# Stick-breaking attention: a head pair's weighted sums on both array column halves, logits on both row halves

## The reference

```python
kb, vb = k_sh[:, :, :end], v_sh[:, :, :end]
logits = jnp.einsum("bhtd,bhsd->bhts", q[:, :, s0:end], kb) * (Dh ** -0.5)
mask = s_idx[None, :] < t_idx[:, None]
log_keep = jnp.where(mask, jax.nn.log_sigmoid(-logits), 0.0)
after = jnp.sum(log_keep, axis=-1, keepdims=True) - jnp.cumsum(log_keep, axis=-1)
wts = jnp.where(mask, jnp.exp(jax.nn.log_sigmoid(logits) + after), 0.0)
outs.append(jnp.einsum("bhts,bhsd->bhtd", wts, vb))
```

## Time and profile before

| | us |
|---|---|
| median of 3 runs | 1438.62 |
| lowest, highest | 1436.43, 1439.15 |
| span of the profiled execution | 1436.6 |
| the attention, first logits to the last weighted sum | 769.5 to 916.0 |

### The profile page before, as it was taken

One profiled execution on the slowest core, in us unless ns is written; L12 is line 12 of the kernel. 1 busy time (PEld: TensorE's weight loads), 2 busy tenths in 40 slices (PEclk: granted clock), 3 DMA queues, 4 the chain that ended last, 5 costly groups with the idle time before them and its releaser, 6 DMA issues.

```text
span 1436.6 us, 17837 instructions
## 1 busy us (share of the span) xinstructions
PE 1348.6 (94%) x7266; PEld 1037.2 (72%) x7266; DVE 472.6 (33%) x844; ACT 565.2 (39%) x926; POOL 398.5 (28%) x162
## 2 busy tenths in 40 slices
PE   6699999999999988999998999898999999999979
PEld 3588867789888866777775555676887777777747
DVE  0755532342342321334221333213112233242541
ACT  3343458432233522344344566323313434553410
POOL 0343431311124443233332000033223313335131
PEclk9899999999999989999999999999999999999969
DMA  9333311234442012222312000022213321224001
GB/s 334 110 88 104 100 59 59 89 118 147 137 129 89 2 59 88 71 85 83 109 64 88 0 0 1 1 88 94 88 53 109 93 70 60 88 71 179 16 0 59
DMA packets 102978, 117.82 MB, mean 82 GB/s; under 512 B 4560, under 2 KB 88944, under 8 KB 102904
## 3 DMA queue, kind: packets, MB, share of 16 engines
q1 hardware_dynamic: 98640, 112.21, 24.0%
q10 hardware_dynamic: 4264, 4.57, 1.1%
HBM read 111.52 MB, written 2.10 MB: 79 GB/s over the span
## 4 chain that ended last, share of the span: by engine, by line
PE 86%; ACT 6%; DVE 5%; issue 2%; ACTq 0%; DMA 0%; DVEq 0%
PE ps L1541 46%; PE ps L1635 4%; PE ps L2054 3%; PE ps L1769 3%; PE ps L1917 3%; PE ps L1784 3%; PE ps L1930 2%; PE ps L1903 2%; PE ps L1782 2%; PE ps L1624 2%; PE ps L1920 2%; PE ps L2023 1%; PE ps L1851 1%; PE ps L1846 1%; PE ps L2010 1%
## 5 line engine op out<-in xcount | busy, mean ns | idle before, releaser
L427 POOL TENSOR_TENSOR wlo<-raw,whi 128x2048 fp32r<-128x2048 f32 x58 | 267.2, 4607 | 697.5 <-ACT whi L550 685.1
L550 ACT ACTIVATE whi<-raw 128x2048 fp32r<-128x2048 f32 x56 | 106.9, 1911 | 264.6 <-PE ps L1541 229.6
L1635 PE MATMUL ps<-work,cs 128*128 128x512 f32 x160 | 78.4, 610 | 4.3 <-ACT work L555 4.1
L578 ACT ACTIVATE rbuf<-ps,cs 128x512 f32<-128x512 f32 x59 | 40.0, 679 | 63.4 <-PE ps L1635 48.7
L435 POOL TENSOR_TENSOR wlo<-raw,whi 128x2048 fp32r<-128x2048 f32 x10 | 46.3, 4634 | 66.8 <-ACT whi L614 66.8
L1314 DVE SCALAR_TENSOR_TENSOR nlk<-ps,att 128x1280 f32<-128x1280 f32 x16 | 23.9, 1492 | 118.9 <-ACT att L851 118.9
L444 POOL COPY yib<-cs 128x512 f32<-128x512 f32 x40 | 24.1, 615 | 122.6 <-PE ps L1784 122.6
L1784 PE MATMUL ps<-XT,yib 128*128 128x128 f32 x320 | 57.7, 276 | 0.0
L1541 PE MATMUL ps<-hC_hi,whi 128*128 128x512 f32 x208 | 55.1, 407 | 0.0
L939 ACT ACTIVATE p<-sc,nmx 128x256 f32<-128x256 f32 x64 | 32.1, 502 | 57.8 <-DVE nmx L1382 57.8
L1917 PE MATMUL ps<-nlk,cs 128*128 128x512 f32 (+3 forms) x128 | 48.1, 458 | 6.0 <-DVE after L1324 6.0
(11 more groups left out here) (367 smaller groups left out, 2972.1 us busy)
## 6 DMA issues: line engine op xcount, KB each, us to landing
raw<-in_w_in_dram SPq DMA_DIRECT2D x24, 1024.0 KB, 5.2
raw<-in_w_in_a_dram SPq DMA_DIRECT2D x16, 1024.0 KB, 5.6
raw<-in_w_ada_dram SPq DMA_DIRECT2D x16, 1024.0 KB, 5.2
raw<-in_w_ada_kv_dram SPq DMA_DIRECT2D x8, 1024.0 KB, 5.5
raw<-in_w_kv_dram SPq DMA_DIRECT2D x8, 1024.0 KB, 5.2
raw<-in_w_in_b_dram SPq DMA_DIRECT2D x8, 1024.0 KB, 5.4
ada_a<-in_w_ada_dram SPq DMA_DIRECT2D x4, 1024.0 KB, 8.3
ada_b<-in_w_ada_dram SPq DMA_DIRECT2D x4, 1024.0 KB, 10.7
```

The costliest lines, as they stand in the source:

```text
L427: pool.tensor_tensor(wlo[:, s, :], raw[:, s, :], whi[:, s, :].bitcast(F32), ALU.subtract).then_inc(lo_ready, 1)
L550: A(whi[:, s, :], raw[:, s, :], ACT.Copy).then_inc(hi_ready, 1)
L578: A(rbuf[:, g % 2, :], ssbank(g), ACT.Ln, scale=1.0 / width, bias=epsc).then_inc(ss_read, 1)
L1635: mm(ssbank(g), stat, work4[:, n % 4, :], start=first, stop=last).then_inc(sq_used, 1)
```

## The change

- `weighted` now takes a pair: for each j the product of the even head and then that of the odd head. It is called on odd n alone, `weighted((n - 3) // 2)`, and counts pairs in `pv_full`. `att` has four buffers instead of three, and the waits on `pv_full` on ScalarE and VectorE follow.
- New tiles `swk`, `swq` hold, for the pair at hand and in two buffers, the keys of blocks 1 and 3 and the queries from 128 on with the partition halves exchanged. SP copies them there with four DMA transfers for a pair (64 KB of keys and 96 KB of queries for each half), `swap(kt)`, after the load of half 0 of `D_OUTB + 1` and before that of half 1.
- `qk` computes blocks j = 0 and 2 on the head's own row half and j = 1 and 3 on the other half from the copies, in the order 0, 1, 2, 3. It waits for the copies, and once for both weights of head n - 2 before j = 0.
- Memory: `att`, `nlk1`, `after0` and `after1` now lie over half 1 of `whi` and `wlo`. So half 1 of `D_OUTB` is split after the attention: ScalarE's `next_hi(D_ZB + 1, 1)` moves behind the loop, ahead of the last `yb_hi`; POOL waits for 7 pairs before its part; SP's load of half 1 of `D_OUTB + 1` waits for that.

```diff
+            def swap(kt):
+
+                sp.wait_ge(kqn_done, 8 + kt + 1)
+                sp.wait_ge(dense_full, 4 * (D_VB + 2))
+                if kt >= 2:
+                    sp.wait_ge(qk_full, 2 * (kt - 2) + 2)
+                for e in range(2):
+                    to, of = slice(64 * e, 64 * e + 64), slice(64 - 64 * e, 128 - 64 * e)
+                    sp.dma_start(swk[to, kt % 2, :, :],
+                                 kTb[of, kt, :].rearrange("p (a two n) -> p a two n", two=2, n=128)[:, :, 1, :]
+                                 ).then_inc(swapped[kt % 2], 16)
+                    sp.dma_start(swq[to, kt % 2, :], qTb[of, kt, 128:512]).then_inc(swapped[kt % 2], 16)
...
+                if r == load_of["dense", D_OUTB + 1]:
+                    load(r, (0,))
+                    for kt in range(KD):
+                        swap(kt)
+                    load(r, (1,))
+                    continue
...
                 for s in range(2):
+                    if (d, s) == (D_OUTB, 1):
+                        pool.wait_ge(pv_full, KD - 1)
                     split_lo(d, s)
...
-            copies(D_ZB + 1, lambda j: zsT[:, 4 + j, :], gate_done, ACT.Silu)
+            next_hi(D_ZB + 1, 0)
+            for j in range(4):
+                act.wait_ge(dense_full, 4 * (D_ZB + 1) + j + 1)
+                A(zsT[:, 4 + j, :], dense[j], ACT.Silu).then_inc(gate_done, 1)
...
             def head_exps(n):
-                a = att[:, n % 3, :]
+                a = att[:, n % 4, :]
                 act.wait_ge(qk_full, n + 1)
-                if n >= 3:
-                    act.wait_ge(pv_full, n - 2)
+                if n >= 4:
+                    act.wait_ge(pv_full, (n - 4) // 2 + 1)
...
+            next_hi(D_ZB + 1, 1)
             yb_hi(KD - 1)
...
             def qk(n):
-                s, kt, rs = n % 2, n // 2, slice(64 * (n % 2), 64 * (n % 2) + 64)
-                for j in (0, 1, 3, 2):
-                    if n >= 2 and j < 2:
-                        pe.wait_ge(wt_done, 2 * (n - 2) + 1 + j)
-                    last = mm(logit_cols(s, off[j], 512 - 128 * j), kTb[rs, kt, 128 * j:128 * j + 128],
-                              qTb[rs, kt, 128 * j:512], start=j != 3, stop=True, skip_group_check=True)
+                s, kt = n % 2, n // 2
+                rs, other = slice(64 * s, 64 * s + 64), slice(64 - 64 * s, 128 - 64 * s)
+                pe.wait_ge(swapped[kt % 2], 64 * (kt // 2 + 1))
+                if n >= 2:
+                    pe.wait_ge(wt_done, 2 * (n - 2) + 2)
+                for j in (0, 1, 2, 3):
+                    if j % 2:
+                        k, q = swk[other, kt % 2, j // 2, :], swq[other, kt % 2, 128 * j - 128:384]
+                    else:
+                        k, q = kTb[rs, kt, 128 * j:128 * j + 128], qTb[rs, kt, 128 * j:512]
+                    last = mm(logit_cols(s, off[j], 512 - 128 * j), k, q, start=j != 3, stop=True,
+                              skip_group_check=True)
...
-            def weighted(n):
-                s, kt, rs = n % 2, n // 2, slice(64 * (n % 2), 64 * (n % 2) + 64)
-                pe.wait_ge(wt_done, 2 * n + 2)
-                if kt >= 2 and n % 2 == 0:
+            def weighted(kt):
+                pe.wait_ge(wt_done, 4 * kt + 4)
+                if kt >= 2:
                     pe.wait_ge(yb_done, kt - 1)
                 for j in range(NT):
-                    last = mm(ps[rs, 6 + kt % 2, 128 * j:512], Vb[:, j, 64 * n:64 * n + 64],
-                              att[:, n % 3, off[j]:off[j] + 512 - 128 * j], start=j == 0, stop=True, skip_group_check=True)
+                    for n in (2 * kt, 2 * kt + 1):
+                        rs = slice(64 * (n % 2), 64 * (n % 2) + 64)
+                        last = mm(ps[rs, 6 + kt % 2, 128 * j:512], Vb[:, j, 64 * n:64 * n + 64],
+                                  att[:, n % 4, off[j]:off[j] + 512 - 128 * j], start=j == 0, stop=True,
+                                  skip_group_check=True)
                 last.then_inc(pv_full, 1)
...
-                if n >= 2:
-                    weighted(n - 2)
+                if n >= 3 and n % 2:
+                    weighted((n - 3) // 2)
                 if n + 1 < HB:
                     qk(n + 1)
```

More of the change, by code:

```diff
@@ L137, in mixer_stack @@
             with ExitStack() as s2:
-                att = sb("att", [128, 3, 1280], F32, s2)
-                after1 = sb("after1", [128, 256], F32, s2)
-            with ExitStack() as s2:
                 sc2 = sb("sc2", [128, 2, 512], F32, s2)
@@ L157, in mixer_stack @@
             kbg = sb("kbg", [128, 2, 4, 128], F32, scope)
+        with ExitStack() as scope:
+            sb("pad_w0", [128, 2048], F32, scope)
+            nlk1 = sb("nlk1", [128, 1280], F32, scope)
+            after0 = sb("after0", [128, 384], F32, scope)
+            sb("pad_w1", [128, 3200], F32, scope)
+            att = sb("att", [128, 4, 1280], F32, scope)
+            after1 = sb("after1", [128, 256], F32, scope)
         hold = sb("hold", [128, 12288])
@@ L194, in mixer_stack @@
             zsT = sb("zsT", [128, KD, T], F32, B)
-            nlk = sb("nlk", [128, 2, 1280], F32, B)
+            nlk0 = sb("nlk0", [128, 1280], F32, B)
             ybt = sb("ybt", [128, 2, 512], F32, B)
-            after0 = sb("after0", [128, 384], F32, B)
-            pad_b = sb("pad_b", [128, KD * T - 3968], F32, B)
+            swk = sb("swk", [128, 2, 2, 128], F32, B)
+            swq = sb("swq", [128, 2, 384], F32, B)
+            sb("pad_b", [128, KD * T - 3584], F32, B)
             with ExitStack() as s2:
@@ L238, in mixer_stack @@
             vst = sb("vst", [128, 2, 512], F32, Cc)
+        nlk = (nlk0, nlk1)
         ps = ctx.enter_context(nc.psum_tensor("ps", [128, 8, 512], F32))
@@ L336, in mixer_stack @@
         os_done = sem("os_done")
+        swapped = [sem(f"swapped{s}") for s in range(2)]
         v_moved = [sem(f"v_moved{s}") for s in range(2)]
@@ L362, in raw_free, with load @@
                 sp.wait_ge(ada_done if what == "ada" else lo_ready, 2 * n + s + 1)
-            def load(r):
+            def load(r, halves=(0, 1)):
                 what, n = order[r]
-                for s in range(2):
+                for s in halves:
                     if r:
@@ L854, in head_weights @@
                 act.wait_ge(sfx_full, n + 1)
-                A(att[:, n % 3, cols], logits(n % 2)[:, cols], ACT.Exp).then_inc(wt_done, 1)
+                A(att[:, n % 4, cols], logits(n % 2)[:, cols], ACT.Exp).then_inc(wt_done, 1)
             def logits(s):
@@ L1296, in yb @@
             def yb(kt):
-                dve.wait_ge(pv_full, 2 * kt + 2)
+                dve.wait_ge(pv_full, kt + 1)
                 if kt == 0:
@@ L1313, in _ @@
                     dve.wait_ge(sfx_full, n - 1)
-                STT(nlk[:, s, :], logits(s), 0.0, att[:, n % 3, :], ALU.max, ALU.add).then_inc(nlk_done, 1)
-                k1, k3, k2 = nlk[:, s, 512:896], nlk[:, s, 896:1024], nlk[:, s, 1024:1280]
+                STT(nlk[s][:, :], logits(s), 0.0, att[:, n % 4, :], ALU.max, ALU.add).then_inc(nlk_done, 1)
+                k1, k3, k2 = nlk[s][:, 512:896], nlk[s][:, 896:1024], nlk[s][:, 1024:1280]
                 dve.wait_ge(nlk_done, n + 1)
@@ L1913, in suffix_sums @@
                 pe.wait_ge(after_done, n + 1)
-                later = {0: after0[:, :], 1: after1[:, :], 2: nlk[:, s, off[3]:off[3] + 128]}
+                later = {0: after0[:, :], 1: after1[:, :], 2: nlk[s][:, off[3]:off[3] + 128]}
                 for j in range(NT):
                     width = 512 - 128 * j
-                    last = mm(logit_cols(s, off[j], width), C("negtri"), nlk[:, s, off[j]:off[j] + width],
+                    last = mm(logit_cols(s, off[j], width), C("negtri"), nlk[s][:, off[j]:off[j] + width],
                               start=False, stop=True, skip_group_check=True)
```

## The result

The changed kernel takes 1453.32 us (median of 4 runs, 1452.38 to 1456.83), the kernel before 1437.53 in the same series: a ratio of 1.0111, 95% interval 1.0096 to 1.0126. It is 15.8 us slower, outside the predicted range.

A forecast was written before the change was run, and what follows sets the result against it. TensorE's 8.49 us a round was taken as the attention's bound, with a 7.98 us chain under it. Gain -6.6, clock +7.4, start 0 and end 0 gave +0.8 on 1438.62: 1439.4 us, range 1432 to 1444.5.

The forecast's parts named there:

- The stage's chain: Attention: suffix sums, first weights, Ln, nlk, small sums, next suffix sums; 7.98 us a round, under TensorE's 8.49.
- logits with mask: Attention, on TensorE: with both row halves in use, one head's logits and mask take 1.64 us instead of 2.58.
- the stall of even rounds: Attention: TensorE idles 2.5 us in each even round, its logits waiting for ScalarE's second weights.
- the full-clock gain: Attention: 13 rounds shorten by 0.51 us each, 6.6 us gained while the clock is full.
- rival (f): Attention matmuls: only neighbours overlap, rounds are 8.2 us, the gain 3.9; +3.5 us in all, 1442; chance 0.04.
- the number of falls: Attention: the clock falls after 4.5 of seven even stalls, 1.65 us each, 7.4 us lost; bounds 0 and 12.2.
- Rival (b): Attention: the clock falls at nearly every uncovered stall; seven falls cost 12.2; +3.3 to +6 us, 1443.5; chance 0.17.
- all seven: Attention: a clock fall after every one of the seven even stalls was listed as a sign that the prediction is wrong.
- The end: 0: After the attention: the last sums and moved split cost nothing, POOL's part having 9 us of cover before the output projection.
- The start: 0: Start of attention: copies land at 770.5, Abs of head 0 stays about 772.5; bounds 1.0 gained, 2 lost.
- (c): Start or end of attention: copies land late or the moved split delays the output projection; +3 to +5, 1443; chance 0.05.
- Rival (d): Attention matmuls: the halves stand in line instead of running side by side; +18 us, 1457; chance 0.02.

The follow-up runs named there:

- e3: Changed kernel with two extra, unneeded 512-column products filling the stall of each of the seven even rounds: 1438.36 us, ratio 1.0006 to the kernel before.
- e2: Changed kernel with POOL's moved split waiting for VectorE's last yB_lo ("split later"): 1448.63 us, ratio 1.0073 to the kernel before.
- e1: Changed kernel with the swapped copies of pairs 0 and 1 queued ahead of the raw load ("copies first"): 1449.65 us, ratio 1.0086 to the kernel before.
- e9: Changed kernel with two extra products in each even stall, first copies ahead of the raw load, POOL's split after the last yB_lo: 1430.42 us, ratio 0.9962.
- e10: Changed kernel with one extra 512-column product instead of two in each even round's stall: 1442.3 us, ratio 1.0045 to the kernel before.
- e4: Changed kernel with each head's weighted sums by themselves again, logits on both row halves kept: 1439.05 us, ratio 1.0013 to the kernel before.
- e6: Changed kernel with ScalarE's Ln of head n ahead of both weights of head n-1: 1428.13 us, ratio 0.9939 to the kernel before.
- e7: Changed kernel with Ln ahead of the weights, first copies ahead of the raw load, POOL's split after the last yB_lo: 1417.43 us, ratio 0.9868.
- e12: Changed kernel with Ln ahead of the weights, POOL's split after the last yB_lo, logits on the head's own half, no copies: 1426.81 us, ratio 0.9927.
- e5: Changed kernel with pairs' sums kept, but logits on the head's own row half with the old order and waits, no copies: 1454.49 us, ratio 1.0124.
- e8: Kernel before with ScalarE's Ln of head n ahead of the weights of head n-1: 1434.63 us, ratio 0.999 to the kernel before.

## Why the prediction was wrong

**Right.** The stage's chain (7.98 forecast, 8.03 measured); the pair's sums (2.3, 2.38); logits with mask (1.64, 1.69); the stall of even rounds (2.5, 2.64); the full-clock gain, 6.6 us forecast, 13 x (8.49 - 8.03) = 6.0 measured. Row and column halves run side by side, and one half's queue doesn't wait for the other's. The rule of the Trainium skill (TensorE: Matmul & The Clock Gate, What overlaps and what doesn't) that matmuls start and end in strict program order, from which rival (f) was made, fails here: after 788.65 the timeline has block 3 on the other half at 789.40 and block 2, which stands before it in the program, at 789.58.

**The failed step: the number of falls**, "I take 4.5 falls of 7, at 1.65 us each". All seven even stalls were followed by a fall, and two of these lasted through the logits and the suffix sums both (849 to 856, 904 to 911). The rounds lost 117.1 - 104.3 = 12.8 us to the clock (e3), where 7.4 were put down. I had counted three stalls of four in the trace of before and marked them down for the dense work on both sides. Seven falls of seven, and none once the stalls are filled (e3), show that this work is no protection. The count had a slip too: the stall "of over a microsecond" at 786 was two, of 0.69 and 0.74 us, so the old trace already had a fall behind stalls much shorter than the new ones. Rival (b) named this with a chance of 0.17 and a cost of 12.2, and "all seven" was one of the prediction's own signs of being wrong.

**Falls outside the rounds** were not in the sum at all: the last round (+1.66), the last suffix sums (5.42 us from the first start to the last end instead of 3.72, +1.69), the first stretch of the projection (+1.16). A stall was priced only where the diff puts it. The 2.0 us before the last suffix sums was there before and forgiven once; in the changed kernel it was not.

**"The end: 0" failed for a reason the step never asked about.** The cover for POOL's split was worked out from who waits for its result (9 us, and there is one: in e2 the split ends inside the first unit). What it runs beside was not looked at. It stood next to two VectorE operations with two SBUF inputs on the path: +3.57 us (5.83 for 2.26; e2 gives 2.27).

**"The start: 0" was a term too small.** The copies landed at 770.5, as forecast, but all work ahead of them ended 1.3 us earlier in this execution, and the load with copies behind it took 5.9 us to land, not 5.1: 7.1 us from load to copies where I had 5.9. The wait of 3.07 us then cost clock as well, so the logits took 2.59 us and not 1.46. Together +2.54, and by e1 3.7 us up to the second suffix sums, since the split that used to hold Abs is gone. So the upper bound, 2, was too small as well.

So the sum, by the prediction's terms: the gain of 6.6 measured 7.8 (112.1 to 104.3: 6.0 at full clock, and the 1.74 of the fall at 788 that the kernel before had in these rounds); the clock cost 12.8 in the rounds and 4.5 behind them; start and end cost 6.7 in place of 0 (2.54 + 0.72, and 5.17 - 1.69). With the -2.2 of everything else (1.3 of it ahead of the attention; no run explains it) that is the 14.0. Of the rivals, (b) and (c) had been named apart, each small; they came together. Rival (d), +18, was nearest in time and wrong: nothing stood in line.

## What to carry to other kernels

Freed TensorE time is worth only what the next chain leaves: find the round where the freed work is missing (here the last one, 7.98 against 8.49), and shorten that chain in the same change, or the gain can turn into stalls that cost clock. A stall on TensorE is priced with a fall of the clock behind it until a run shows otherwise, and dummy products in the stall are a cheap run to learn it (15 us here). For an instruction moved elsewhere ask both who waits for it and what it will run beside; and put small copies that something waits for ahead of the large load in the same queue.

## What was not expected of the hardware

The stall's length did not sort the falls. After 2.64 us the clock fell in 7 of 7 even rounds, in the changed kernel as in e1 and e2. After the equal stall of the first round it did not fall in six kernels (changed, e1, e2, e3, e9, e10) and in one it did (e4). After 1.70 to 1.78 us it fell in 3 of 21 rounds (e6 none, e7 one, e10 two), after 0.92 us in none of 14 (e3, e9). But after 0.91 us with logits on one row half behind it, it fell in 2 of 7 (e12), and two stalls of 0.69 and 0.73 us with such logits between them (e5) again lost some 12.6 us in 13 rounds. Logits on one row half are not enough for it either: behind the 0.69 us of e8's first round the clock held.

Once there were falls, they came in the same places. Three kernels whose attention begins at different times show, in one profiled execution each, the same rounds to 0.05 us (starts of suffix sums in the timelines):

| | rounds from the second suffix sums on, us |
|---|---|
| changed kernel | 8.20 9.50 8.76 8.91 9.35 8.32 9.56 9.61 8.65 9.02 9.24 8.43 9.56 |
| copies first | 8.19 9.50 8.75 8.91 9.35 8.31 9.56 9.61 8.65 9.02 9.24 8.42 9.56 |
| split later | 8.19 9.53 8.72 8.94 9.32 8.35 9.56 9.62 8.62 9.04 9.21 8.45 9.56 |

The falls come once for each pair of heads in all three. In these executions chance has little part in it, so it could not be averaged away, as my 4.5 of 7 had assumed.
